# A mixture-of-experts loop in 25 visits of two or three experts, instead of 32 visits of two

## The reference

```python
s = sigmoid(t @ w_router)                      # 256 tokens x 64 experts
sel = s + b_router                             # best 4 of 8 groups of experts, then the best 8 experts
gates = s of the 8 chosen, divided by their sum, x 2.5
hid = silu(t @ w_gate[e]) * (t @ w_up[e])      # 1024 -> 256, for each expert e
routed = sum over e of (hid * gates[:, e]) @ w_down[e]   # 256 -> 1024
out = routed + (silu(t @ ws_gate) * (t @ ws_up)) @ ws_down   # the shared expert
```

## Time and profile before

| what | us |
|---|---|
| three timed runs | 1362.43, 1364.97, 1365.32 (median 1364.97) |
| profiled execution, first to last instruction | 1362.6 |
| PE busy | 1292.4 (95%) |
| DVE busy | 497.4 (37%) |
| ACT busy | 328.1 (24%) |
| chain that ended last: PE | 89% of the span |
| all DMA traffic | 497.53 MB, 365 GB/s on average |

### The profile page before, as it was taken

How to read it: one execution, slowest core, us unless ns; L and a number is a source line. 1 busy time by engine, 2 the same in 40 slices (tenths; PEclk the granted TensorE clock), 3 DMA queues, 4 the chain that set the end, 5 groups by cost and what they waited for, 6 DMA issues and landing times.

```text
span 1362.6 us, 25006 instructions
## 1 busy us (share of the span) xinstructions
PE 1292.4 (95%) x9570; PEld 656.0 (48%) x9570; DVE 497.4 (37%) x1280; ACT 328.1 (24%) x596; POOL 73.5 (5%) x91
## 2 busy tenths in 40 slices
PE   3898988999999999999989987999999999999997
PEld 2675754444444444444448775444444444444443
DVE  0645474223322322322346465523223223223323
ACT  1523541111111111111144364111111111111112
POOL 0230020000000000000033002000000000000000
PEclk8899999999999999999999998899999999999999
DMA  9689566999999999999985946499999999999993
GB/s 364 255 330 398 205 287 237 412 419 420 422 421 422 422 422 422 422 422 422 422 324 183 372 165 253 170 380 416 421 421 422 422 422 422 422 421 422 422 422 157
DMA packets 86302, 497.53 MB, mean 365 GB/s; under 512 B 7728, under 2 KB 7728, under 8 KB 36336
## 3 DMA queue, kind: packets, MB, share of 16 engines
q1 hardware_dynamic: 84416, 491.58, 88.4%
q0 software_dynamic: 1840, 5.31, 1.0%
HBM read 494.24 MB, written 2.62 MB: 365 GB/s over the span
## 4 chain that ended last, share of the span: by engine, by line
PE 89%; DMA 4%; DVE 2%; ACT 2%; SPq 1%; issue 1%; POOL 0%; DVEq 0%; ACTq 0%
PE PS L898 32%; PE PS L929 17%; PE PS L693 12%; PE PS L876 10%; PE PS L891 8%; DMA weights<-in_w_in 3%; PE PS L837 2%; PE PS L714 2%; DMA weights<-in_w_ada 1%; PE PS L917 1%; PE PS L867 1%; SPq L394 1%; PE PS L883 1%; PE PS L665 1%; PE PS L789 1%
## 5 line engine op out<-in xcount | busy, mean ns | idle before, releaser
L898 PE MATMUL PS<-weights,gathered 128*32 128x512 f32 (+1 forms) x3968 | 451.3, 592 | 0.0
L898 PEld LDWEIGHTS PS<-weights,gathered 128*32 128x32 f32 (+1 forms) x3968 | 133.6, 111 | 306.3 <-issue 305.1
L929 PE MATMUL PS<-weights,hiddenT 128*32 128x512 f32 (+1 forms) x1984 | 233.0, 595 | 0.0
L1598 DVE SCALAR_TENSOR_TENSOR hidden<-PS,slot_gate,silu 128x256 f32<-128x256 f32 x64 | 31.0, 484 | 387.6 <-ACT silu L1137 387.6
L876 PE MATMUL PS<-pick_rows,x_parts 128*128 128x512 f32 (+2 forms) x576 | 148.2, 400 | 2.1 <-DVE pick L1544 1.9
L1144 ACT ACTIVATE y_hi<-PS 128x512 fp32r<-128x512 f32 x128 | 76.4, 597 | 293.3 <-PE PS L929 293.3
L876 PEld LDWEIGHTS PS<-pick_rows,x_parts 128*128 128x128 f32 x576 | 100.7, 188 | 76.5 <-issue 58.5
L1608 DVE TENSOR_TENSOR y_lo<-PS,y_hi 128x512 fp32r<-128x512 f32 x128 | 88.5, 691 | 114.0 <-ACT y_hi L1144 114.0
L1137 ACT ACTIVATE silu<-PS 128x256 f32<-128x256 f32 x64 | 24.5, 383 | 411.3 <-PE PS L898 411.3
L693 PE MATMUL PS<-weights_split,hT_high 128*128 128x512 f32 x448 | 111.8, 405 | 9.3 <-ACT hT_high L990 7.3
L929 PEld LDWEIGHTS PS<-weights,hiddenT 128*32 128x32 f32 (+1 forms) x1984 | 60.5, 110 | 121.5 <-issue 114.6
(11 more groups left out here) (268 smaller groups left out, 981.6 us busy)
## 6 DMA issues: line engine op xcount, KB each, us to landing
weights<-in_w_gate SPq DMA_DIRECT2D x128, 1024.0 KB, 11.4
weights<-in_w_up SPq DMA_DIRECT2D x128, 1024.0 KB, 15.4
weights<-in_w_down SPq DMA_DIRECT2D x128, 1024.0 KB, 13.9
weights<-in_w_ada SPq DMA_DIRECT2D x24, 2048.0 KB, 12.3
weights<-in_w_in SPq DMA_DIRECT2D x9, 2048.0 KB, 11.2
weights<-in_w_out SPq DMA_DIRECT2D x4, 2048.0 KB, 15.3
weights<-in_w_in SPq DMA_DIRECT2D x2, 1024.0 KB, 23.7
weights<-in_ws_gate SPq DMA_DIRECT2D x2, 1024.0 KB, 4.7
```

What stands on the lines that cost most here:

```text
L898: last = mm(PS[a:z, 4, :].rearrange("p (a n) -> p a n", a=2), xgT[:, b, j, a:z], w[:, e, :, j, :], start=j == 0, stop=j == KT - 1, tile_po ...
L929: last = mm(PS[a:z, bank, :], hidT[:, j, a:z], w[:, e, j, n * HALF:(n + 1) * HALF], start=j == 0, stop=j == FT - 1, tile_position=(0, a), ...
L1598: v.scalar_tensor_tensor(hid[:, :], PS[:, 4, F:2 * F], slot_gate[:, b % 2:b % 2 + 1], silu[:, :], ALU.mult, ALU.mult)\
```

## The change

A layer has 25 visits. The four fixed experts keep the first two visits of 64+64 slots. The two heaviest others get 96 slots and a visit each, with a light expert of 32. Then seven rounds follow, of three visits and eight experts: 64+32+32, 64+32+32 and 64+64 slots; four experts of a round come from ranks 3 to 30 of the sort, four from the lighter 30. Experts with more tokens than slots would come in extra rounds.

The weights lie in four places of one expert each. SP loads expert k into the place of expert k-4, waiting per place: within a round of experts 0 to 7, waits stand ahead of 0, 2, 4 and 7, first for the gate and up loads of a visit's experts, then for their down loads. Expert 2 of a round, the third of its first visit, takes the place of an expert of the visit just before.

Gathers run three visits ahead. Ahead of the first gate/up all rows of the two fixed visits are gathered at once (32 matmuls), the second set of gathers is gone, and `shared_down` is moved behind the fourth visit, adding to what the visits accumulated. The shared down weights have a place of their own and are loaded when the table is ready. The first loads of the next layer wait for the down multiplication of the last visit but one.

The core of the diff, with the small tables and DVE's and ACT's index arithmetic left out:

```diff
-PAIRS = N_EXP // 2
-AHEAD = 4
-FIXED_CAP, HEAVY_CAP, LIGHT_CAP = 64, 96, 32
+AHEAD = 3
+CAP, TOP_CAP, LIGHT_CAP = 64, 96, 32
+FIRST = {-1: (TWO, (0, 1)), 0: (TWO, (2, 3)), 1: (TOP, (4, 5)), 2: (TOP, (6, 7))}
+ROUND = {0: (THREE, (0, 1, 2)), 1: (THREE, (3, 4, 5)), 2: (TWO, (6, 7))}
+SLOTS = 4
+GATHERED = ((0, 1, 2), (3, 4, 5), (6, 7))
+ROUNDS = (N_EXP - 8) // 8
...
-    return out + spare + [("shared_gu",), ("shared_dn",)]
+    return out + spare + [("shared_gu",)]
...
@@ SP
-                count = sp.value_load(n_visits[0:1, 0:1], min_val=PAIRS, max_val=VISITS)
-                with sp.Fori(2, count, 2) as i:
-                    for b in range(2):
...
-                        sp.wait_ge(L[l]["gu_mm"], i + (b - 1))
-                        load_pair(sp, l, b, experts, ("w_gate", "w_up"))
-                        sp.wait_ge(L[l]["down_mm"], i * 2 + 2 * (b - 1))
-                        load_pair(sp, l, b, experts, ("w_down",))
+                sp.wait_ge(sht_mm, l + 1)
                 sp.wait_ge(table_ready, l + 1)
+                sp.dma_start(shared_down_w[:, :], rows(io["ws_down"][l])).then_inc(shared_in, 16)
...
+                for visit, ks in ((0, (4, 5)), (1, (6, 7))):
+                    experts = {k: expert_of(k - 4) for k in ks}
+                    freed("gu_mm", visit + 1)
+                    for k in ks:
+                        load_expert(sp, l, k, experts[k], ("w_gate", "w_up"))
+                    freed("down_mm", 2 * (visit + 1))
+                    for k in ks:
+                        load_expert(sp, l, k, experts[k], ("w_down",))
+                with sp.Fori(1, last_round) as q:
+                    before = {0: 0, 1: 0, 2: 1, 3: 1, 4: 2, 5: 2, 6: 2, 7: 3}
+                    for _, ks in ROUND.values():
+                        experts = {k: expert_of(q * 8 + (k - 4)) for k in ks}
+                        for name, names in (("gu_mm", ("w_gate", "w_up")), ("down_mm", ("w_down",))):
+                            each = 1 if name == "gu_mm" else 2
+                            for k in ks:
+                                if k in (0, 2, 4, 7):
+                                    freed(name, q * (3 * each) + before[k] * each)
+                                load_expert(sp, l, k, experts[k], names)
@@ PE, ahead of the loop
-                for odd in range(2):
-                    gather(odd, 1, 5 + odd, 0)
-                    gather(2 + odd, 2, 5 + odd, P).then_inc(S["ga_mm"], 1)
+                for js, bank in (((0, 1, 2), 5), ((3, 4), 6), ((5, 6), 0), ((7,), 1)):
+                    n = 1 if bank == 5 else 2
+                    for k, j in enumerate(js):
+                        last = gather(j, 0, n, bank, k * n * P)
+                    last.then_inc(S["ga_a"], 1)
                 overflow_places()
...
                 scatter_prep(0)
-                shared_down()
-                for b in range(AHEAD):
-                    visit(0, b, FIXED_TILES if b < FIXED else TILES)
+                shared_hidden_out()
+                items()
+                pe.wait_ge(shT_ready, l + 1)
+                for b, (form, ks) in FIRST.items():
+                    visit(0, b, form, ks)
+                shared_down()
...
@@ DVE
-                step(v.tensor_tensor(RK[:, :, 0:NULL].rearrange("p g (r e) -> p g r e", r=REGIONS),
...
+                step(v.tensor_scalar(RK[:, :, 0:N_EXP], rk[:, :, :], -1000.0, None, ALU.add))
...
                 shared_hidden(1)
+                dve.wait_ge(S["put_mm"], 1)
+                slots_of(0, TWO)
+                step(v.tensor_tensor(RK[:, :, N_EXP:].rearrange("p g (r e) -> p g r e", e=N_EXP),
...
                 dve.wait_ge(over_mm, l + 1)
```

More of the change, by code:

```diff
@@ L93, in const_layout @@
     for name, n in (("ident", P), ("cos", 64), ("sin", 32), ("band", 4 * P), ("before", 64),
-                    ("slot", HEAVY_CAP), ("place", 2 * VISITS), ("caps", REGIONS * N_EXP), ("key_row", 2 * N_EXP),
-                    ("expert", 7), ("earlier", P), ("minus_half", 4),
+                    ("slot", TOP_CAP), ("rank_at", LIST), ("over_at", LIST - OVER_AT), ("starts", REGIONS),
+                    ("key_row", 2 * N_EXP), ("expert", 5), ("earlier", P), ("minus_half", 4),
                     ("pick32", 32)):
@@ L409, in _ @@
[L409 to L421 removed]
+                    block_done(sp, last - RING + 3 * b)
@@ new lines, in visit @@
+                def visit(q, b):
+                    t, js = of_round(q, 3, b + 1), GATHERED[(b + 1) % 3]
+                    act.wait_ge(S["gu_mm"], t + 1)
+                    run(silu[:, :], PS[:, 4, 0:F], ACT.Silu).then_inc(S["silu_done"], 1)
+                    act.wait_ge(S["ga_a"], t + 5)
+                    last = gathered(js[0:1], 0, AHEAD, 5)
+                    if b < 0:
+                        last = gathered((6, 7), 2, 3, 0)
+                    if len(js) == 3:
+                        act.wait_ge(S["ga_c"], of_round(q, 2, {-1: 1, 0: 2, 2: 3}[b]))
+                        last = gathered(js[2:3], 0, AHEAD, 7)
+                    last.then_inc(S["xg_a"], 1)
+                    act.wait_ge(S["ht_mm"], t + 1)
+                    run(hidT[:, :, :], PS[:, 4, 0:F].rearrange("p (j s) -> p j s", j=FT), ACT.Copy).then_inc(S["hidT_done"], 1)
@@ L1150, in _ @@
-                with act.Fori(AHEAD, count, AHEAD) as i:
-                    for b in range(AHEAD):
-                        visit(i, b)
+                last_round = act.value_load(n_visits[0:1, 0:1], min_val=ROUNDS + 1, max_val=MOST_ROUNDS + 1)
+                with act.Fori(1, last_round) as q:
+                    for b in ROUND:
+                        visit(q, b)
                 act.wait_ge(acc_done, NG * l + 1)
@@ L1592, in _ @@
[L1592 to L1604 removed]
+                dve.wait_ge(cleared, 2 * (l + 1))
@@ L1612, in _ @@
-                count = dve.value_load(n_visits[0:1, 0:1], min_val=PAIRS, max_val=VISITS)
-                with dve.Fori(AHEAD, count, AHEAD) as i:
-                    for b in range(AHEAD):
-                        visit(i, b, HEAVY_CAP)
+                for b in FIRST:
+                    visit(0, b, FIRST[b + 1][0] if b < 2 else THREE)
+                last_round = dve.value_load(n_visits[0:1, 0:1], min_val=ROUNDS + 1, max_val=MOST_ROUNDS + 1)
+                with dve.Fori(1, last_round) as q:
+                    for b in ROUND:
+                        visit(q, b, ROUND[(b + 1) % 3][0])
```

452 lines of the change are left out of this document (229 added, 223 removed).

## The result

| | before | after |
|---|---|---|
| median (4 runs each), us | 1364.82 | 1392.37 (1385.34 to 1396.29) |
| ratio, 95% interval | | 1.0196 (1.0161 to 1.0230) |
| profiled execution, us | not on record | 1389.67 |
| its span, us | 1362.6 | 1387.9 |

A forecast was written before the change was run, and what follows sets the result against it. It took the DMA stream to bound the loop at heart, PE by a hair. Two layers at -4.1 us, -0.8 for a wait and +1.2 for clock gave 1354.8 of span, plus 2.4: 1357.2 us, range 1346 to 1372.

The forecast's parts named there:

- What bounds: Expert loop: the DMA stream at heart (14.95 us a visit), PE (14.7) by a hair and its lead.
- rivals 1 and 4: Rival 1: PE is the bound, 1159 us, chance 0.01; rival 4: DMA stream faster, 1347 with no cold start, chance 0.13.
- Steady rounds: Rounds of eight experts: 12.5 us queued against 9.1 needed, margin 3.3 us in three-expert visits, so no holes.
- The clock: Gate/up after PE waits: 2.4 us lost a visit, under the margin inside the loop, added once at a layer's last visit.
- rival 2: Rounds: cold clock lengthens gate/up after each wait, the stream runs dry twice a round, kernel slower; chance 0.20.
- its own sign: Rounds: one taking clearly longer than 59.8 us, with a DMA share under 1, would show the cold clock breaking the stream.
- Its condition: Rounds: each wait must leave gate/up longer by more than 3.3 us for the cold clock to break the stream.
- its two prices, 1373 and 1409: Whole kernel with the stream broken by the cold clock: 1373 us with 3.8 us lost, 1409 with 5 lost.
- Start: First layer: first gate/up begins at about 215.1 us and ends at 222.0, not 232.2, 10.2 us sooner.
- First visits: First layer's four opening visits: gate/up of the first ends at 222.0 us, of visit 4 at 264.8.
- Holes of the start: Each layer's stream start: holes of 2.9 us near 264 and 4.1 near 284, together 7.0.
- The layer's sum: First layer: stream from 223.6 plus 448.5, holes and tail; loop ends at 691.8 us against 695.9 before, -4.1.

The follow-up runs named there:

- e_quarter: The kernel after with a quarter of each down weight loaded, in fact for experts 4 to 7 of each round alone: 1376.35 us, ratio 1.0082.

## Why the prediction was wrong, point by point

- **What bounds: right.** The stream takes over when PE has less to do. Without holes a round takes 59.86 us, forecast 59.8, and the rate is the old 421 GB/s. PE as the bound, and a faster stream (rivals 1 and 4), are out. What the prediction lacks is a second bound as long as the first, the chain of waits of some 59.7 us with cold gate/ups (e_quarter).
- **Steady rounds: the step that failed.** "When the third expert of a visit lands, three down loads and one gate/up are queued behind it: 7.5 + 5.0 = 12.5 us", a margin of 3.3, "so no holes, unless gate/up gets longer by 3.3". The term that was too large is the 12.5 us as a time at full rate. The five loads do land 12.4 us behind, but the full rate ended 9.9 us behind the landing (344.13 to 354.0), since a landing comes with the last of the 16 DMA engines (the 16 small packets that close the last load end between 354.29 and 356.08), and the others are by then through with it. In the packets of the trace this is so in both layers: in the 24 three-expert visits of rounds 2 to 7 the last of the five loads landed 12.4 us behind, and in 20 of them the DMA share fell below 0.9 at 8.8 to 11.8 us. The 12.5 was 2.6 us too long, and the margin at the place shown was 3.3 - 2.6 = 0.7 us.
- **The clock: right in size, wrong in what it does.** The forecast was 2.4 us lost in a visit; the mean of the 13 is 9.1 - 7.1 = 2.0 (1.3 to 2.7). "Inside the loop it stays under the 3.3 of margin" is false with a margin of 0.7: on average up to 1.3 us of hole at each of the two three-expert visits of a round, and 61.5 - 59.9 = 1.6 us a round were measured. The Trainium skill's rule ("TensorE: Matmul & The Clock Gate", section "HAM oscillation — how this bites in real kernels") that each burst behind a wait starts at the lower level again was cited and set aside as too cheap; the trace agrees with it in 13 of the 21 visits behind the first four (waits of 5.0 to 7.1 us), and in the seven third visits (waits of 1.0 to 3.5 us) gate/up did not start cold. So rival 2 came true in its mechanism, and its own sign was there, a round clearly over 59.8 us with a DMA share of 0.99. Its condition, more than 3.3 us lost, was not met; that 1392 lies between its two prices, 1373 and 1409, is luck.
- **Start: 3.2 us late.** First gate/up ended at 225.19, not 222.0: 1.4 of it a later begin (216.48, not 215.1), 1.8 the cold clock (8.71 us), which had even odds.
- **First visits: 1.3 us longer.** The fourth gate/up ended 44.1 us behind the first (225.19 to 269.31), where 42.8 were counted: the first visit has 20 gather matmuls (3.3 us), not 8, and a wait for ACT (0.62).
- **Holes of the start: 7.8, forecast 7.0.** Right in number, place and nearly in size; the second one is shared down's, as its removal showed.
- **The layer's sum.** From the first round's gate/up at 284.40, not 279.5 (+4.9), over six rounds of 61.5, not 59.8 (+10.1), and from the seventh round's gate/up to the last matmul 55.7 us instead of 53.5 (+2.2): 709.0 instead of 691.8. The last matmul of the first loop, the line that answers to the earlier trace rows:

```profile
705.35 3.65 PE L973 MATMUL PS<-weights,hiddenT 128*64 128x512 f32 x16
```

The second layer loses about as much again (the span grew by 25.3 us, 13.1 of them up to this line). That matmuls in the waits and shared down behind the fifth visit bring 1358.06 us, next to the 1357.2 of the forecast, is luck too: in that kernel the first gate/up ends at 223.99, not 222.0, and the start holes are 3.4 us, not 7.0.

## What to carry over

Count a buffer's margin up to the moment at which the rate falls (here 9.9 us), not up to the landing of the last transfer that is queued (12.4), and count it against the slowest form of the consumer: here PE came back from waits of 5 to 7 us at the lower clock. The change turned the bound engine into a waiting one, and that engine became slower per piece of work, 9.1 us for 7.1; where its end gates the next transfer, this goes into the transfer's time. Six useless matmuls cost nothing in a wait of 5 to 7 us, and 5.4 us where data lay ready: place them visit by visit.

## What the runs showed of the hardware that was not expected

- Behind a wait of 6.15 us TensorE ran at 0.50 for some 5.2 us of gate/up and then at 1.00 (rows 344 to 354). Six 128x512 matmuls (5.4 us) in such waits kept these gate/ups at 7.07 us: a granted clock of 0.99 over 380 us, against 0.90.
- The 16 DMA engines do not finish together: of five 1 MiB loads queued behind a landing the last landed 12.4 us after it, but the rate broke off after 9.9 us (434 to 270 GB/s, share 0.65).
- With an eighth of a round's stream left out, at the same order of waits, a round took 59.7 us, the full stream's pace, at a DMA share of 0.91: a chain of waits of the same length stood beside the stream.
